# Four score buffers in the windowed attention, earlier norm vectors, and a ratio split between two engines

## The reference

```python
def diff_attention(...):                       # C
    lam = exp(sum(lq1 * lk1)) - exp(sum(lq2 * lk2)) + lambda_init
    sc = einsum('bhmqd,bhmsd->bhmqs', qb, k) * scale + bias      # two maps m per head
    p = softmax(sc, axis=-1)
    a = p[:, :, 0] - lam * p[:, :, 1]
    o = rms_norm(einsum('bhqs,bhsd->bqhd', a, v), g_head) * (1.0 - lambda_init)

def neighbourhood_attention(...):              # D: 8 rows x 16 columns of a 16 x 64 grid
    sc = einsum('bqhd,bqnhd->bhqn', qb, kb) * scale + take(bias_flat, rel)
    o = einsum('bhqn,bqnhd->bqhd', softmax(sc, axis=-1), vb)

mix = concatenate([oa, ob, oc, od], axis=-1) @ w_out[l]   # oa, ob, od normalized with g_out_*
x = x + rms_norm(mix, norm_mix_post[l])
```

## Time and profile before

| | us |
|---|---|
| median of 3 runs | 3023.75 (3023.37 to 3025.94) |
| profiled execution | 3023.84 |
| its span | 3022.0 |
| busy: PE, DVE, ACT, POOL | 2740.4 (91%), 1931.9 (64%), 1385.5 (46%), 553.4 (18%) |

### The profile page before, as it was taken

The page is one execution under the profiler, slowest core; times in us unless marked ns, Lnnn a source line. Parts: engine busy times, 40 slices in busy tenths (PEclk is TensorE's granted clock), DMA queues, the critical chain, the costliest instruction groups (busy, mean ns, idle before and its releaser), DMA issues. The chain is left out here.

```text
span 3022.0 us, 37758 instructions
## 1 busy us (share of the span) xinstructions
PE 2740.4 (91%) x13872; PEld 2286.0 (76%) x13872; DVE 1931.9 (64%) x2856; ACT 1385.5 (46%) x2330; POOL 553.4 (18%) x487
## 2 busy tenths in 40 slices
PE   5998899887979999999879979988869799999997
PEld 4986888566758887888769859876658588878886
DVE  5612867886678887445774148669766888864457
ACT  4312766776343322443433147668654433334344
POOL 2122514780000000000021225248500000000000
PEclk7999999898989999999989989989989899999998
DMA  7232655543224444855533326754412244467555
GB/s 210 60 136 84 207 147 177 83 99 112 63 63 153 154 154 157 274 195 194 182 83 100 120 86 202 191 153 64 136 50 77 87 150 152 152 215 234 195 186 169
DMA packets 326941, 431.08 MB, mean 143 GB/s; under 512 B 82006, under 2 KB 207706, under 8 KB 326492
## 3 DMA queue, kind: packets, MB, share of 16 engines
q1 hardware_dynamic: 326736, 428.56, 46.1%
q10 hardware_dynamic: 12, 0.02, 0.0%
HBM read 288.00 MB, written 140.86 MB: 142 GB/s over the span
## 5 line engine op out<-in xcount | busy, mean ns | idle before, releaser
L1997 PE MATMUL f_ps<-dn_g 128*128 128x512 f32 x2688 | 617.1, 391 | 10.0 <-DVE dn_g L2228 10.0
L1997 PEld LDWEIGHTS f_ps<-dn_g 128*128 128x128 f32 x2688 | 505.4, 189 | 117.8 <-DVE dn_g L2228 7.2
L2228 DVE TENSOR_TENSOR dn_g<-dn_raw,dn_g 128x2048 fp32r<-128x2048 f32 x112 | 256.4, 2291 | 265.2 <-ACT dn_g L2077 265.2
L1987 PE MATMUL f_ps<-hc_h,up_w_h 128*128 128x512 f32 x896 | 352.5, 393 | 25.9 <-DVE up_w_l L2194 20.5
L2077 ACT ACTIVATE dn_g<-dn_raw 128x2048 fp32r<-128x2048 f32 x112 | 214.3, 1915 | 331.8 <-PE f_ps L1997 215.9
L1987 PE MATMUL f_ps<-hc_h,up_w_l 128*128 128x512 f32 x896 | 351.7, 393 | 0.0
L1987 PEld LDWEIGHTS f_ps<-hc_h,up_w_h 128*128 128x128 f32 x896 | 170.3, 190 | 63.1 <-DVE up_w_l L2194 27.5
L1987 PE MATMUL f_ps<-hc_ld,up_w_h 128*128 128x512 f32 x512 | 200.4, 391 | 0.0
L1987 PEld LDWEIGHTS f_ps<-hc_h,up_w_l 128*128 128x128 f32 x896 | 170.1, 190 | 35.8
L490 POOL TENSOR_TENSOR w_row_l<-w_row_first,w_row_h 128x512 fp32r<-128x512 f32 x12 | 14.9, 1281 | 904.4 <-ACT w_row_h L599 904.4
L1275 DVE CUSTOM_DVE_ANT_0 s_ps_c<-s_ps_c,distance 128x1024 f32<-128x1024 f32 x128 | 156.7, 1225 | 12.3 <-PE s_ps_c L1158 12.3
(11 more groups left out here) (297 smaller groups left out, 6461.7 us busy)
## 6 DMA issues: line engine op xcount, KB each, us to landing
act_blocks<-u_stage SPq DMA_DIRECT2D x32, 1792.0 KB, 6.6
dn_raw<-act_blocks SPq DMA_DIRECT2D x112, 512.0 KB, 3.9
mix<-in_w_down SPq DMA_DIRECT2D x128, 256.0 KB, 3.5
down_sums<-mix SPq DMA_DIRECT2D x128, 256.0 KB, 2.8
up_raw<-in_w_up SPq DMA_DIRECT2D x32, 1024.0 KB, 5.3
dn_raw<-down_sums SPq DMA_DIRECT2D x64, 512.0 KB, 4.8
dn_raw<-in_w_down SPq DMA_DIRECT2D x48, 512.0 KB, 4.6
w_raw<-in_w_in SPq DMA_DIRECT2D x16, 512.0 KB, 4.1
```

Of the source, the lines that this page charges most:

```text
L1987: last = nc.tensor.matmul(dst, wt[:, x % RING, k, :], tok, start=(opens[j] and k == 0 and i == 0), stop=(k == KT // 2 - 1 and i == 2), ski ...
L1997: last = nc.tensor.matmul(f_ps[:, bank0[pi] + i, :], lhs[:, n % 4, 0, q, i * P:(i + 1) * P], rhs[:, n % 4, 1, q, :], start=(down_opens[pi] ...
L2228: nc.vector.tensor_tensor(g_l[:, n % 4], dn_raw[:, n % 3], g_h[:, n % 4], ALU.subtract) \
```

## The change

In D: a stage of its own (`window_stage`) with four score buffers of 512 columns and four probability buffers, another order of work and further lookahead. In D's SyncE program the eleven small loads are added behind the weights; they leave the output stage. In C: ScalarE multiplies the first sum by lambda, VectorE only makes the reciprocal, GpSimd's scaling takes both as columns.

```diff
@@ C, ScalarE @@
+                    def scale_sum(n):
+                        if n == 0:
+                            act.wait_ge(S["lam_done"], 1)
+                        act.wait_ge(S["exp_done"], 2 * n + 1)
+                        nc.scalar.activation(ratio[:, 1, n:n + 1], z[:, 0, n:n + 1], ACT.Copy, scale=lam) \
+                            .then_inc(S["lam_scaled"], 1)
...
                         if n + 1 < n_all:
                             exponential(n + 1, 1)
+                            scale_sum(n + 1)
@@ C, GpSimd @@
                         pool.wait_ge(S["ratio_done"], n + 1)
-                        nc.gpsimd.tensor_scalar(second[:, n % 2, :], second[:, n % 2, :], ratio[:, 1, n:n + 1], 1.0,
-                                                ALU.mult, ALU.mult).then_inc(S["scaled"], 1)
+                        pool.wait_ge(S["lam_scaled"], n + 1)
+                        nc.gpsimd.tensor_scalar(second[:, n % 2, :], second[:, n % 2, :], ratio[:, 1, n:n + 1],
+                                                ratio[:, 0, n:n + 1], ALU.mult, ALU.mult).then_inc(S["scaled"], 1)
@@ C, VectorE: weigh(n) @@
-                        after(nc.vector.reciprocal(ratio[:, 0, n:n + 1], z[:, 1, n:n + 1]))
-                        nc.vector.scalar_tensor_tensor(out=ratio[:, 1, n:n + 1], in0=z[:, 0, n:n + 1], scalar=lam,
-                                                       in1=ratio[:, 0, n:n + 1], op0=ALU.mult, op1=ALU.mult) \
-                            .then_inc(S["ratio_done"], 1)
+                        nc.vector.reciprocal(ratio[:, 0, n:n + 1], z[:, 1, n:n + 1]).then_inc(S["ratio_done"], 1)
@@ D: window_stage, a copy of attention_stage but for these (then orders of TensorE, ScalarE, VectorE) @@
+            DEEP = 4
+                prob = mem.take("prob_d", [P, DEEP, 3 * P])
+                s_ps = ps(c, "s_ps_d", [P, DEEP, HALF])
...
+                    for n in range(DEEP):
+                        scores(n)
+                    for n in range(n_all + 4):
+                        if n < n_all:
+                            turn(n)
+                        if n + DEEP < n_all:
+                            scores(n + DEEP)
+                        if 0 <= n // 2 - 1 < n_groups:
+                            values(n // 2 - 1, n % 2)
+                        if n >= 4 and n % 2 == 0:
+                            finish(n // 2 - 2)
...
+                    exponential(0)
+                    exponential(1)
+                    for n in range(n_all + 2):
+                        if n + 2 < n_all:
+                            exponential(n + 2)
+                        if n < n_all:
+                            high(n)
+                        if n >= 3 and n % 2 == 1:
+                            lift(n // 2 - 1)
...
+                    for n in range(3):
+                        maximum(n)
+                    for n in range(n_all + 4):
+                        if n + 3 < n_all:
+                            maximum(n + 3)
+                        if n < n_all:
+                            low(n)
+                        if n >= NT + 3 and (n - 3) % NT == 0:
+                            divide((n - 3) // NT - 1)
@@ D, SyncE: fetch_out, behind the eight loads of w_out @@
+                for j, name in ((0, "g_out_a"), (1, "g_out_b"), (3, "g_out_d")):
+                    for r in range(2):
+                        sp.dma_start(g_col[:, 2 * j + r:2 * j + r + 1], col(vec(name, r * P, (r + 1) * P))) \
+                            .then_inc(S["const_landed"], 16)
+                for j in range(2):
+                    for r in range(2):
+                        sp.dma_start(g_col[r * HD:(r + 1) * HD, 4 + j:5 + j], col(vec("g_out_c"))).then_inc(S["const_landed"], 16)
+                sp.dma_start(out_li[:, :], row_vector(vec("lambda_init"))).then_inc(S["const_landed"], 16)
                 sp.wait_ge(S["w_landed0"], 16 * KT)
+                sp.wait_ge(S["const_landed"], 16 * 11)
@@ output stage, VectorE (the same eleven loads leave its SyncE program) @@
+                    nc.vector.tensor_scalar(g_col[:, 4:6], g_col[:, 4:6], out_li[:, 1:2], None, ALU.mult) \
+                        .then_inc(S["gain_done"], 1)
                     mix_sums(0)
-                    dve.wait_ge(S["const_landed"], 16 * 11)
-                    nc.vector.tensor_scalar(g_col[:, 4:6], g_col[:, 4:6], li[:, 1:2], None, ALU.mult) \
-                        .then_inc(S["gain_done"], 1)
                     mix_norm(0)
```

More of the change, by code:

```diff
@@ L104 @@
  s_done hc_hi hc_lo p1_copied p5_copied p7_added relu11 posts_done staged u_stored0 u_stored1
- evac_done taken tile_done final_done""".split()
+ lam_scaled lam_done evac_done taken tile_done final_done""".split()
 class Sems:
@@ L1237, in _ @@
                     exponential(0, 1)
+                    scale_sum(0)
                     for n in range(n_all + VALUE_LAG):
@@ L1308, in _ @@
                     after(nc.vector.tensor_tensor(lam, lam, li[:, 0:1], ALU.subtract))
+                    dve.sem_inc(S["lam_done"], 1)
                     for n in range(n_all + VALUE_LAG + 1):
@@ L1356, in build @@
             wo_raw = arena((104, 136)).take("wo_raw", [P, KT, D])
+            oc = arena((136, 137))
+            g_col = oc.take("o_g_col", [P, KT])
+            out_li = oc.take("o_li", [P, 2])
             W = HD // 2
@@ L1509, in fetch_out @@
                     sp.dma_start(wo_raw[:, k, :], a["w_out"][layer][k * P:(k + 1) * P, :]).then_inc(S["w_landed0"], 16)
+                col = lambda v: v.rearrange("a p -> p a")
+                for j, name in ((0, "g_out_a"), (1, "g_out_b"), (3, "g_out_d")):
+                    for r in range(2):
+                        sp.dma_start(g_col[:, 2 * j + r:2 * j + r + 1], col(vec(name, r * P, (r + 1) * P))) \
+                            .then_inc(S["const_landed"], 16)
+                for j in range(2):
+                    for r in range(2):
+                        sp.dma_start(g_col[r * HD:(r + 1) * HD, 4 + j:5 + j], col(vec("g_out_c"))).then_inc(S["const_landed"], 16)
+                sp.dma_start(out_li[:, :], row_vector(vec("lambda_init"))).then_inc(S["const_landed"], 16)
                 sp.wait_ge(S["w_landed0"], 16 * KT)
+                sp.wait_ge(S["const_landed"], 16 * 11)
             def bias(i):
@@ L1519, in build @@
                      [lambda x0, x1, h=h: DK_S[:, h, x0:x1]] * 2, DV_S[:, :, h, :]) for h in range(NHEAD)]
-            attention_stage("d", arena((-38, -24), (80, 104)), maps, tiles,
-                            lambda m: slice((12 + m) * HD, (13 + m) * HD), mix, fetch_out, 16)
+            window_stage(arena((-38, -24), (80, 104)), maps, tiles,
+                         lambda m: slice((12 + m) * HD, (13 + m) * HD), mix, fetch_out, 16)
             h_f = arena((-64, -32)).take("h_f", [P, KT, SEQ])
@@ L1530, in build @@
                 w_l = arena((104, 136)).take("ow_l", [P, KT, D], F32R)
-                om = arena((0, 48), (80, 92), (136, TOP))
+                om = arena((0, 48), (80, 92), (137, TOP))
                 w_h = om.take("ow_h", [P, KT, D], F32R)
@@ L1540, in build @@
                 g_pre = om.take("o_g_pre", [P, D])
-                g_col = om.take("o_g_col", [P, KT])
-                li = om.take("o_li", [P, 2])
                 ss = om.take("o_ss", [P, 4, 4])
@@ L1561, in _ @@
                 def _(sp):
-                    col = lambda v: v.rearrange("a p -> p a")
-                    for j, name in ((0, "g_out_a"), (1, "g_out_b"), (3, "g_out_d")):
-                        for r in range(2):
-                            sp.dma_start(g_col[:, 2 * j + r:2 * j + r + 1], col(vec(name, r * P, (r + 1) * P))) \
-                                .then_inc(S["const_landed"], 16)
-                    for j in range(2):
-                        for r in range(2):
-                            sp.dma_start(g_col[r * HD:(r + 1) * HD, 4 + j:5 + j], col(vec("g_out_c"))).then_inc(S["const_landed"], 16)
-                    sp.dma_start(li[:, :], row_vector(vec("lambda_init"))).then_inc(S["const_landed"], 16)
                     def residual(t):
```

125 lines of the change are left out of this document (added).

## The result

The changed kernel takes 2996.26 us (median of 4 executions, 2995.74 to 3001.38), the kernel before 3023.56 us on the same chip (4, 3022.53 to 3025.94). The ratio is 0.9912, with an interval from 0.9895 to 0.993: 27.3 us or 0.9% faster. The forecast was 2995.8.

The account below looks back on a forecast made before the run. VectorE was taken to pace C, TensorE's stalls to cost time in D, and a small-load wait to hold the output stage's head. Terms -12.0 - 7.0 - 9.0 = -28.0 took 3023.84 to 2995.8 us; range 2986 to 3008.

Parts of the forecast that it names:

- Part 1: Head of the output stage: no wait for eleven small loads, now hidden in D; 5.4 and 6.6 us, -12.0 us.
- Part 2: Stage C: VectorE loses the product and the wait for its reciprocal; pace 3.82 to 3.68 us, -7.0 us.
- 25 x 0.14 = 3.5: Stage C: 25 periods a pass, each 0.14 us shorter, 3.5 us a pass; six earlier periods left as they are.
- my list of loops: Stage C: VectorE's sum 3.56 us, first-maximum loop 3.64, ScalarE 3.65 to 3.75 with a lift, GpSimd 3.67 to 3.72.
- Rival (c): Stage C: GpSimd's two-column scaling takes 2.37 us instead of 1.12, kernel slower at 3068 us; chance 0.04.
- Part 3: Stage D: transposes, scores four ahead, then values on TensorE cover its stalls; 4.5 us a pass, -9.0 us.
- 12 x 0.38 = 4.6: Stage D: 12 of 14 TensorE waits for the low part go, 0.38 us each, 4.6 us a pass.
- The margin of 0.05 us: Stage D: TensorE's work of 1.71 us just covers the 1.66 us chain through ScalarE and VectorE.
- rival (a): Stage D does not come apart and gives 0.86 us a pass at most; total -21, 3003 us; chance 0.16.
- The term 0.86: Head of D: two more scores issued while TensorE waits for the value load, 0.86 us a pass.
- Rival (d): TensorE's clock dip in D stays away or moves with shorter idle: 2991 or 3000 us; downwards chance 0.08.
- The case in which both C and D fail: Something of D not coming apart and C's gain being lost, together -14 us; chance 0.05.

Follow-up runs that it names:

- part 1 alone: Against the kernel before: only the eleven small loads moved from the output stage into D; ratio 0.9961, 11.8 us of 3021.8.
- The three parts alone: Three kernels, each the kernel before with one part of the diff: moved small loads 0.9961, C's change 0.9977, new stage D 0.9977.
- The last experiment: Changed kernel plus a one-column VectorE operation with two SBUF inputs between C's two low parts, in the middle of GpSimd's sum; 3097.87 us, ratio 1.0259.

## Why the prediction was right, and where it was not

**Part 1 was right in each step.** -12.0 was forecast and -12.1 measured: 5.45 and 6.62 us by the two waits, 5.4 and 6.6. The small loads hid in D. With part 1 alone D grew by 0.4 to 0.6 us: in the first pass the first values start 8.59 us into D instead of 8.29, and the other 0.3 comes behind the third pair. Whether the loads account for that stays open: the clock's rows are much alike in both, and lengths of D differ by as much from execution to execution.

**Part 2: mechanism right, size too small.** The term was 25 x 0.14 = 3.5 a pass. The 25 periods from 562.25 to 655.97 took 93.72 us instead of 97.96, 4.24, which is 0.17 each. The pace fell to 3.65, not 3.68: I had averaged in ScalarE's iterations with a lift at up to 3.75, and the scalings are 3.63 to 3.67 apart in all of the 25 without a change of head. Another 0.45 to 0.5 came from the iterations that I had left as they are. The scaling was priced at nothing extra and takes 0.08 more; the constant put back gave 0.2 to 0.3 us a pass, so that price hardly counted. Of my list of loops, VectorE's sum came out longer than 3.56, with 0.15 us from the start of the reciprocal to that of the next maximum, and the loop of 3.65 through the first exponential, TensorE and the second maximum was not on the list at all. That its value is nearly one of the numbers I had (3.64) is chance.

The rows of the scaling are these (groups of GpSimd in C; busy us, mean ns), and it was 1120 ns with the constant:

```profile
L1265 POOL TENSOR_SCALAR second_c<-second_c,ratio_c 128x1024 f32<-128x1024 f32 x32 | 38.4, 1199 | 36.1 <-DVE ratio_c L1292 36.1
```

Rival (c), a scaling at 2.37, is excluded by it. The Trainium skill (GPSIMD Engine Reference, "Elementwise — side-by-side cycle accounting") has a one-tensor body with up to two operations at about one cycle an element, from which I had taken that a second column costs next to nothing. The trace agrees but for 0.08 us on 1.12.

**Part 3: the pairs two thirds right, the head not at all, and C's change left out of D.** Two terms were too large, and a third was missing.
- The term 12 x 0.38 = 4.6 became 3.15. Over one head before and after, four pairs took 2.72, 3.01, 3.04 and 3.36 us and take 2.66, 2.61, 2.64 and 3.20 (second pass). Two of the four gained 0.40, about the 0.38 that I had written. The pair with the short tiles lost a stall of 0.06 only, because it had hardly one, and the pair with the divide kept most of its own (3.20): there the divide's 0.69 us on VectorE stands ahead of the next maximum, and the fold matmuls wait for it. I had taken the count of waits times one pair's loss, where each kind of pair has to be read by itself. The margin of 0.05 us was enough, so rival (a) is out.
- The term 0.86, two scores in the shadow of the value load, became 0.2 in D alone (14.86 to 14.62 us up to the third pair's values; 14.83 to 14.57 in the second pass) and 0.3 to 0.5 behind the changed C. The work did move into the shadow, but what ends the shadow is the load: the first values start 8.29 and 8.20 us after D's beginning before, 8.05 and 8.39 after, and TensorE only stands idle longer (2.72 us instead of 2.23).
- The effect of C's change on D had no term. Behind the shorter C the old D is 1.2 us longer in each pass, at another clock. Rival (d) had the right cause, but tied it to the wait for the load in D and not to C. The split load and the busy end of C show what the clock costs in the head: 2.3 to 2.4 us a pass behind the load, 0.8 to 1.0 before it.

Against the kernel before, the head of the full change is 0.6 to 0.8 us longer, the 1.2 less what the new order gives. Since heads with the same instructions took from 14.05 to 15.77 us, these shares of a few tenths are those of the profiled executions and no more.

**What holds for the sum.** -28.0 was forecast and -27.3 measured, with errors of -2.4 and +4.1 in C and D and 0.9 in the rest of the output stage. The three parts alone give 11.8, 7.0 and 6.9, together 25.7, and the full change 26.6 by its ratio, the same within the intervals. But C's change alone pays 2.4 of its 9.4 us back in D in its profiled execution. That the total came within 1 us of the forecast is luck: what D lacked, 4.1, was nearly made up for by what C gave beyond its term and by 0.9 in a stretch that nobody had changed. The case in which both C and D fail (-14, some 3010) was given a chance and lies outside the range that I had stated; it didn't come to that.

**The exclusion.** I had used the product's 0.92 us for 0.1 us and a part of a chance. The last experiment shows it in each iteration that has the operation. The rule of the Trainium skill (SBUF — State Buffer, "SBUF: two separate sides") is that a VectorE operation with two SBUF inputs and a GpSimd operation exclude each other for a whole instruction. The run agrees, with up to 2.1 us against 0.2.

## What to carry to other kernels

Price a stall by kind of iteration (edge, inner, with the divide), and not by count times one of them; and list the loops that cross three engines and close only after two iterations, since they have no idle time that names them. Where TensorE waits for a load, more work ahead of the wait gave little here (0.2 to 0.5 us of the 0.86 forecast), and a first piece of the load as small as the first use gave 5 us a pass. A shorter stage can move the clock's dips in the next one, so measure the two together. An operation of one column on VectorE with two SBUF inputs takes 0.2 us or up to 2.1, by where it meets GpSimd, so move it to another engine or into GpSimd's gap.

## What the runs showed of the hardware

- TensorE's clock: in the changed kernel it fell to 0.50 (1.2 GHz) with an idle time of 2.7 us and stayed there for some 6 us, though TensorE was busy again; with the same stage and an idle time of 2.67 us in another kernel it came back after 3; with the idle time gone it stayed at 1.00 (2.4 GHz). Twenty transposes that nobody reads, ahead of the barrier, kept it at 1.00 through all of D's head.
- The same stage with the same instructions was longer or shorter by where the dips fell: the old D by 1.2 us after a change in C, the new D by 1.75 us between two passes of one execution.
- Value and weight loads queued together: the piece of a quarter of the values, at the head of the queue, was there by 5.5 us, the whole load at 8.0 us.
- GpSimd's scaling of 128x1024 takes 1120 ns with one column and a constant, 1199 ns with two columns.
- A one-column operation on VectorE in the middle of GpSimd's sum of two tensors took 0.88 us with two tensors from SBUF and 0.19 with one; with two it ended with the sum each time.
